# 160 instead of 144 gathered token rows in the expert stage of a hybrid encoder block

## What is computed

```
q = (h @ w_peer_q).reshape(B, S, PEER_HEADS, 2, PEER_HALF)
s = einsum('bshcd,hckd->bshck', q, peer_keys)
sv, si = top_k(s, PEER_TOPK)                       # 16 of 128 keys, two sides
fv, fpos = top_k(sv[0] + sv[1], PEER_TOPK)         # 16 of 16 x 16 sums
idx, g = si[0] * N_KEYS + si[1] at fpos, softmax(fv)
u = peer_u[idx]                                    # 8 x 16 rows of 2048 a token
act = gelu(einsum('thkd,td->thk', u, h)) * g
out = einsum('thk,thkd->td', act, peer_v[idx])
```

## Time and profile before

| | us |
|---|---|
| runs (3), median | 3813.02 |
| runs, lowest and highest | 3812.77, 3818.5 |
| profiled execution, whole | 3809.69 |
| profiled execution, span of its instructions | 3807.9 |
| PE busy / DVE / POOL / ACT | 3759.3 / 2364.7 / 1702.0 / 1262.9 |

### The profile page before, as it was taken

The page is one execution under the profiler, slowest core; times in us unless marked ns, Lnnn a source line. Parts: engine busy times, 40 slices in busy tenths (PEclk is TensorE's granted clock), DMA queues, the critical chain, the costliest instruction groups (busy, mean ns, idle before and its releaser), DMA issues. The chain is left out here.

```text
span 3807.9 us, 56597 instructions
## 1 busy us (share of the span) xinstructions
PE 3759.3 (99%) x20173; PEld 3446.9 (91%) x20173; DVE 2364.7 (62%) x4027; ACT 1262.9 (33%) x1638; POOL 1702.0 (45%) x1449
## 2 busy tenths in 40 slices
PE   7999999999999998999999999999999999999999
PEld 5778778888888887889999999999999999999999
DVE  5482453000010207886968888888887888888887
ACT  3433453333333323224652222222222222222221
POOL 0444334444444662444015555545553655554223
PEclk9999999999999999999999999999999999999999
DMA  6222112222222322334569998899987898889787
GB/s 205 92 88 100 67 58 98 99 92 95 99 99 92 140 99 104 105 105 151 211 247 330 326 332 318 322 326 334 322 313 281 319 339 311 316 320 340 275 295 249
DMA packets 187946, 800.97 MB, mean 210 GB/s; under 512 B 21024, under 2 KB 59944, under 8 KB 134440
## 3 DMA queue, kind: packets, MB, share of 16 engines
q1 hardware_dynamic: 99776, 492.34, 35.8%
q0 software_dynamic: 83872, 303.22, 22.4%
q10 hardware_dynamic: 4184, 4.01, 0.5%
HBM read 762.39 MB, written 37.09 MB: 210 GB/s over the span
## 5 line engine op out<-in xcount | busy, mean ns | idle before, releaser
L791 ACT ACTIVATE w_hi<-ring 128x1024 fp32r<-128x1024 f32 (+1 forms) x499 | 564.0, 1135 | 1090.1 <-PE bank L1766 718.8
L637 POOL TENSOR_TENSOR p_lo<-ring,p_hi 128x512 fp32r<-128x512 f32 x432 | 563.9, 1306 | 672.5 <-ACT p_hi L791 672.5
L1766 PE MATMUL bank<-h_hi,w_hi 128*128 128x368 f32 (+1 forms) x2304 | 780.3, 339 | 13.1 <-DVE h_lo L1449 7.3
L1766 PE MATMUL bank<-h_lo,w_hi 128*128 128x368 f32 (+1 forms) x2304 | 773.9, 336 | 0.0
L1766 PE MATMUL bank<-h_hi,w_lo 128*128 128x368 f32 (+1 forms) x2304 | 773.7, 336 | 0.0
L1766 PE MATMUL bank<-act_hi,w_hi 128*128 128x368 f32 x2048 | 673.1, 329 | 0.3 <-DVE xT L1640 0.3
L1766 PE MATMUL bank<-act_hi,w_lo 128*128 128x368 f32 x2048 | 672.8, 329 | 0.0
L1766 PE MATMUL bank<-act_lo,w_hi 128*128 128x368 f32 x2048 | 672.8, 328 | 0.0
L757 POOL DMA_INDIRECT grow<-v_rows,g_col x288 | 382.2, 1327 | 516.3 <-DVE g_acc L1621 389.9
L1586 DVE TENSOR_TENSOR w_lo<-ring,w_hi 128x1024 fp32r<-128x1024 f32 x448 | 546.2, 1220 | 77.3 <-ACT w_hi L791 56.6
L791 ACT ACTIVATE p_hi<-ring 128x512 fp32r<-128x512 f32 x464 | 292.7, 632 | 788.7 <-PE bank L1766 784.2
(11 more groups left out here) (219 smaller groups left out, 5056.3 us busy)
## 6 DMA issues: line engine op xcount, KB each, us to landing
ring<-w_exp SPq DMA_DIRECT2D x256, 1024.0 KB
ring<-w_mix SPq DMA_DIRECT2D x64, 1024.0 KB, 4.9
tables<-wt SPq DMA_DIRECT2D x12, 2048.0 KB, 6.8
wg<-tables SPq DMA_DIRECT2D x96, 256.0 KB
ring<-w_qk SPq DMA_DIRECT2D x20, 1024.0 KB, 4.9
ring<-w_o SPq DMA_DIRECT2D x16, 1024.0 KB, 4.9
ring<-w_pq SPq DMA_DIRECT2D x16, 1024.0 KB
xT<-x_t SPq DMA_DIRECT2D x8, 1024.0 KB, 11.9
```

Source lines behind the costliest of these rows:

```text
L637: nc.gpsimd.tensor_tensor(p_lo[:, part, :], ring[slot][:, part, :], p_hi[:, part, :].bitcast(F32), ALU.subtract).then_inc(quarter_lo, 1)
L791: return nc.scalar.activation(out, in_, func, **kw)
L1766: return nc.tensor.matmul(out, lhsT, rhs, start=start, stop=stop)
```

## The change

1. `NX` goes from 16 to 32, so the dense products are 352 wide instead of 368, in all 256 expert tiles. The 32 tokens lie as (token, two heads): 4 partitions a token, 32 row steps each. Row steps are 160 for u and 160 for v instead of 144.
2. 352 tokens are exactly 11 table blocks; the half block in tile 43 goes, with its one-hots, copies and store.
3. 23 row steps a pair instead of 22 (`MORE_DOT` and `MORE_ADD` have seven entries), 6 ahead of the first pair instead of 4, 40 in the tail instead of 28. As 23 is odd and the buffers alternate, DVE's loops hold two pairs in their bodies. The turn from u to v rows takes 10 tiles instead of 5.
4. In `weigh` the 16-wide rest goes. The high part of the activations is made by ACT (`high_act`), not by DVE; the low part (`act_low`) follows behind the second low half of the weights instead of directly.
5. Tables, loads and small arrays are cut or placed anew to fit; four DMAs spread the tokens instead of eight.

```diff
-NX = 16
+NX = 32
-TAIL_MORE = ((), (), (), (0, 3))
-TAIL_LESS = ((4, 6), (4, 6), (5,), (7,))
-MORE_DOT = (2, 5, 8, 10, 12, 14)
+TAIL_MORE = ((0, 7), (0, 7), (0, 7), (0, 1, 2, 4, 5, 6))
+TAIL_LESS = ((4,), (4,), (4,), (7,))
+MORE_DOT = (1, 3, 5, 8, 10, 12, 14)
-FIRST_ROWS = (0, 0, 0, 2, 2)
+FIRST_ROWS = (0, 0, 0, 3, 3)
-N_LOOP = 5
-G_TURN, T_LAST, N_TURN = 6, 5, 10
+N_LOOP = 4
+G_TURN, T_LAST, N_TURN = 6, 10, 7
...
             table_block(NTB // 2 - 1, 0, False)
-            table_block(NTB // 2 - 1, 1, False, 2 * LEFT)
+            table_block(NTB // 2 - 1, 1, False, 0)
...
+            def high_act(g, a, j):
+
+                act_e.wait_ge(act_part, 1 * JG * g + 1 * j + 1)
+                f(act_hi[a][:, j, 0:ND], act_in[a][:, j, 0:ND]).then_inc(act_high, 1)
+
             def expert_pair(g, turn=False):
 
                 for q in range(2 * JG):
                     n = 2 * JG * g + q + R_V
                     halves_ahead(n, q % 2, q if q < JG else None)
+                    if q < JG:
+                        high_act(g, 0, q)
...
             one_hots(NTB // 2 - 1, 0, False)
-            one_hots(NTB // 2 - 1, 1, False, LEFT)
+            low(0, R_TAB + NTB + 1)
...
             def weigh(g, a, j):
 
-                raw, full = act_in[a][:, j, 0:ND], NTB - 1
-                whole = raw[:, 0:full * TB].rearrange("p (a b) -> p a b", a=full)
+                raw, full = act_in[a][:, j, 0:ND], NTU
+                whole = raw.rearrange("p (a b) -> p a b", a=full)
                 v.tensor_tensor(whole, whole, wg[a][:, 0:full, TB * j:TB * j + TB], ALU.mult).then_inc(act_part, 1)
-                rest = raw[:, full * TB:]
-                v.tensor_tensor(rest, rest, wg[a][:, full, TB * j:TB * j + TB - NX], ALU.mult).then_inc(act_part, 1)
-                dve.wait_ge(act_part, 3 * JG * g + 3 * j + 2)
-                v.tensor_copy(act_hi[a][:, j, 0:ND], raw).then_inc(act_part, 1)
-                dve.wait_ge(act_part, 3 * JG * g + 3 * j + 3)
+
+            def act_low(g, a, j):
+
+                raw = act_in[a][:, j, 0:ND]
+                dve.wait_ge(act_high, JG * g + j + 1)
                 v.tensor_tensor(act_lo[a][:, j, 0:ND], raw, act_hi[a][:, j, 0:ND].bitcast(F32), ALU.subtract).then_inc(act_ok, 1)
...
                     low_half(q % 2, n + 2, 1)
+                    if q < JG:
+                        act_low(g, 0, q)
```

More of the change, by code:

```diff
@@ L54 @@
 HT = TB // 4
[L55 to L56 removed]
+NTU = ND // TB
 PAIRS = PH * TOPK
@@ L231, in hybrid_block @@
         g_act = place("g_act", 202, [PAIRS])
-        g_col = [place(f"g_col{i}", 202.5 + i / 16, [2], U32) for i in range(4)]
+        g_col = [place(f"g_col{i}", 202.5 + i / 32, [2], U32) for i in range(4)]
         x_h = place("x_h", 188, [D])
```

86 lines of the change are left out of this document (48 added, 38 removed).

## The result

The changed kernel takes **3859 us** (median of its runs; 3843 to 3873) against 3813 before, a ratio of 1.0114 with a 95% interval of 1.0092 to 1.0135. Forecast were 3762 us and a gain; it is a loss of 46 us. The profiled execution has a span of 3856.6 us, 99.9 more than the 3756.7 of the sum.

A forecast was written before the change was run, and what follows sets the result against it. It took TensorE's columns to bound the expert stage, VectorE and row gathers close behind. 3807.9 - 81.9 - 3.6 + 1.7 + 11 + 18 - 1.7 + 5 + 0.3 = 3756.7 us span, 3762 as median; range 3734 to 3796.

The forecast's parts named there:

- Parts 1 and 2: Expert products 16 columns narrower: -81.9 us; last half block of one-hot table products gone: -3.6, with +1.7 for one-hot waits.
- Part 3: First rows, six instead of four ahead of first pair: TensorE waits of 4 and 8 us, +11 (+3 to +16).
- Part 4: VectorE within pairs: row waits cost 3 us a v pair, 0.4 a u pair; +18 us (0 to 51), less 1.7.
- Rival (b): Every pair: rows' round trip (GpSimd, DMA, four buffers) becomes the bound; 11.7 us gives 3884, 4%; 2% at 11.2 us.
- Part 5: High parts cast by ScalarE, 8 a pair of some 0.48 us: costs 0; without cover 0.5 us a u tile.
- Part 6: Last 8 tiles, 13 rows instead of 9: VectorE ends about 5 us after TensorE; +5 (0 to 8), +0.3 final addition.

The follow-up runs named there:

- the columns' kernel: Changed kernel with the row plan from before (144 rows, last 16 token rows left out), here with five half-row buffers: 3719.8 us, ratio 0.9748.
- the pair of runs with five buffers: Changed kernel with a fifth half-row buffer and loops written out: six rows ahead of the first pair, 3764.5 us; four rows, 3759.9 us.

## Why the prediction was wrong, step by step

**Parts 1 and 2, columns and tables: right.** Tiles came 7.68 us apart, table tiles 15.7 instead of 15.9. With five buffers the columns' kernel has a span 87 us below before (95 by the medians: the profiled executions lie 5 us below the median of before and 3 above that of this kernel); parts 1 and 2 had 84, and pairs of 122.46 instead of 122.9 account for about the rest. The span of that run, 3720.6, is 2 us below what the sum has without its terms for waits, 3722.4. The whole error is in the waits and what goes with them: 34 us forecast, 136 measured. (A slip without weight: with 0.4167 ns a column 13.1 ns don't depend on width, with the 0.415 that stands beside it 13.7.)

**Part 3, the start: right.** PE waits of 4 and 8 us were forecast, 4.16 and 8.18 are there, each with a half clock of 6.8 us (0.76 over 2000 to 2020), twice as long as the 3.4 taken from the earlier trace rows. By the pair of runs with five buffers it is 12.5 us for a forecast of 11. The other 5 us up to the second pair have no shown cause: with the loops written out the second pair begins 5 us sooner, with four buffers (2136.6) as with five (2136.9).

**Part 4, the pairs: this step failed.** I took the 13.3 us that DVE waited for rows in a v pair, added at most the 11 us by which the rows' time shrank, and set the result against DVE's spare time, 3 us a pair and 7.3 at the worst. Measured are 31 us of waits in the v pair shown, and 13.4 us a pair over four v pairs. A wait isn't an amount that stays or grows by a fixed sum: it is what DVE's work leaves of the trips that its row buffers need. The sum to make was rows a pair times trip, against PE's time: 11.5 trips in 122.9 us allow 10.69 us each. The earlier trace rows gave 9.0 and 14.3 us between uses of the same buffer, mean 11.7, but at 128 us a pair a mean of 11.6 follows whether or not the trip is the bound. What the trace of before left open is how much of it was slack; 2.5 us of a trip passed between landing and use, and I took them for free. To fit, 1.15 of them had to go; in the changed kernel's v pairs 0.4 did, and issue, landing and use grew by 0.4. So the trip stayed at 11.85, and 11.5 of these are 136 us. With a fifth buffer the same rows fit into 122.46 us.

**Rival (b) was the truth, and I put it aside with the wrong argument.** It named the mechanism, and 11.7 us a trip gave it 134.6 us a pair and 3884 in all. Against it I held that with 22 rows an 11.7 us trip would make 128.7 us pairs, "where 128.00 stands". 128.7 against 128.00 is no contradiction but the sign that before stood at the very edge: its cushion was used up at the ends of v pairs, PE already waited there, and the last two of its four v pairs took 128.3 and 129.6. Only half of (b) came true, 3859 and not 3884: the u pairs took 122.9 to 127.4 us, with a trip of 10.87.

**Part 5, the high parts: right.** They cost nothing before, and in the changed kernel taking them off DVE saved some 14 us, which its runs' scatter leaves uncertain. It was a relief for the wrong resource, though: in the v pairs shown DVE's work fell by 3 us while its waits for rows rose by 18 (12.8 to 31.0).

**Part 6, the end: right mechanism, a term left out.** PE waits 6.83 us for the last row; 5 us were forecast. But I looked at the last eight tiles only. The 32 tiles behind the pairs hold 40 rows instead of 28, beside the weighing of 32 activation tiles; with the last v pair they cost 45 us over the base where the sum had 8. Moving eight of these rows forward gave 17 us back in these stretches, with five buffers.

**The clock, counted in part 3 and at nothing in parts 4 and 6.** Behind TensorE's waits the granted clock fell to half in the v pairs and at the end as well. The four v pairs of the changed kernel (the rest of its span, at 0.96, stands among the stretches of the result), then both stretches with columns alone and five buffers:

```profile
2897.30:3440.90 543.60, 510.89 (x3072) 504.13 (x3071) 423.38 (x436) 157.38 (x193) 325.98 (x276) 0.97 0.86 310
2859.80:3349.60 489.80, 489.80 (x3074) 489.80 (x3073) 419.05 (x432) 159.89 (x193) 318.43 (x262) 1.00 0.90 334
3349.60:3721.00 371.40, 365.20 (x2304) 364.67 (x2302) 293.73 (x348) 115.06 (x139) 134.44 (x132) 1.00 0.81 297
```

Counted by TensorE's own time over the clock's records, 82 of the 136 us are more idle time and 34 are half clock while it works (4 up to the second pair, 2 in six pairs, 13 in four v pairs, 15 behind them); the other 20 are neither, but products that stood a little further apart. In the v pairs the 13 are hardly a cause: DVE waits there 115.3 us for rows and 1.8 us for another engine, so its work and its row waits make up their length whatever the clock. At the end no run separates the two.

**The range** of 3734 to 3796 missed by 63 us. It took its upper end from the 7.3 us a pair of the same faulty step, and so couldn't see beyond it.

What stays open: why the loops written out, with four buffers, are some 21 us faster than the changed kernel. And POOL's share of the trip: with a quarter of its copies the median was 13 us lower, but its free-to-issue time hardly fell in the v pairs (1.40 us against 1.46), so these 13 us, if they are more than scatter, aren't explained by it.

## What to carry to other kernels

Where work goes round a fixed set of buffers, don't carry its waits over as a sum: divide. Buffers over trip (free, issue, land, and the wait for an in-order engine's turn) is the most items a microsecond; compare it with the rate that the faster kernel will ask for, before and after, and treat equality as the edge. An engine that is busy 77% of the time, as DVE in the 139 us pair, can be the pace setter, and one more buffer, or the same work spaced evenly, then does what taking work off it can't.
